# A product-key expert kernel: the first key's one-hots of four tokens from one bf16 comparison and one product

## The chip, the cores and the metric

The kernel runs on one core of a Trainium2 chip. The metric is the device time of one execution in microseconds. Time before: 1866.86 us, the median of 3 runs (1861.45 to 1871.61).

## The reference

One layer of a hybrid encoder over 512 frames of 1024 features (16 learned meta tokens in front, float32 throughout): a mixer (attention with forget gates beside a state space branch), then a channel mixer with 128 x 128 experts, then a norm. The edit lies in the channel mixer, for half of the tokens:

```
s = einsum('bqhjd,hjnd->bqhjn', qry, keys)          # two halves of the key, 128 scores each
v1, i1 = top_k(s[..., 0, :], 16);  v2, i2 = top_k(s[..., 1, :], 16)
best, pos = top_k(v1 + v2 over all 256 pairs, 16)
e1 = i1[pos // 16];  e2 = i2[pos % 16];  gate = softmax(best)
act = gelu(u[e1 * 128 + e2] . x)
out = sum over 8 heads x 16 picks of gate * act * v[e1 * 128 + e2]
```

So each token has 128 picks (8 heads x 16), each with a first key e1, a second key e2 (both 0 to 127) and a gate.

## The kernel before, in words

The kernel is written against the engines directly: five instruction streams (SyncE `sp`, TensorE `pe`, ScalarE `ac`, VectorE `dve`, GpSimd `pool`), each in program order, ordered against each other by semaphores alone. Nothing is scheduled by a planner. The tokens are handled in two halves. The first 256 gather their experts' rows by indirect DMA. The last 256 (HALF) run densely: all 16384 experts are streamed through TensorE in 128 steps, and a table G[first key, second key, token] of gates weighs the activations. `mul(act, act, G[:, n, :])` (the helper at line 1160) does so in step n.

G is built by the loop that the change edits, once both halves' lists are found. Three transposes bring the picks of a token onto the 128 partitions, so that `first_key`, `second_key` and `gate_chosen` hold 256 columns, one a token (ScalarE copies them out of PSUM, `evac`, line 960). For each token TensorE then multiplies two one-hot matrices, 128 picks x 128 keys each: that of the second key, and that of the first key times the gate. The product is the token's 128 x 128 table.

The loop handles four tokens a group, 64 groups, four groups to a turn of the hardware loop `Fori`, so that keys and gates have addresses from the loop's register (`bass.ds(...)`).

- VectorE (lines 1471 to 1482) compares `numbers` (each of 0..127 four times, bf16) with the four tokens' second keys into `marks[b % 2]`, a bf16 tile laid out key by key with the four tokens side by side (128 x 4 = 512 elements), line 1476. Then it waits for `onehot_free` and makes the first key's one-hot times gate into `oh1[:, b]`, float32, one token an instruction, line 1481.
- ScalarE `widen` (line 1105) turns `marks` token by token into float32 `oh2`, reading at a step of four bf16 elements, that is 8 bytes. `read_gates` (line 1109) copies a group's product from PSUM into G.
- TensorE (line 921) waits for room in PSUM (`gmat_free`), for `oh2_ready` and for `oh1_ready`, and multiplies the group's four tokens; a float32 product is two passes, so 8 matmuls a group. Then it raises `onehot_free`.

`onehot_free` starts at 4, `gmat_free` at 4 and `oh2_ready` at 2, so there are four one-hot buffers and four PSUM banks, and two buffers of marks. SyncE waits for `onehot_free` to reach 4 + 64 before the first expert load (lines 469 and 474), since `u_in` and `v_in`, the tiles it loads into, are the same memory as `oh2` and `oh1`.

Of the kernel before, what the change touches and what calls it, by code (L numbers as in the profile page):

```python
# [15 lines left out]
ALU = mybir.AluOpType  # L16
# [3 lines left out]
BF16 = mybir.dt.bfloat16  # L20
# [3 lines left out]
P = 128  # L24
# [20 lines left out]
HALF = SEQ // 2  # L45
# [67 lines left out]
def hybrid_program(nc, x, meta, g_mix, g_ffn, g_ffn_row, g_out, w_u, w_k, w_q, w_v, w_f, w_g, b_f, b_g, w_att, w_val,  # L113
# [12 lines left out]
    for hf in range(2):  # L126
# [18 lines left out]
        a, b = TILES[hf]  # L145
# [9 lines left out]
    for n, (name, where) in enumerate(order):  # L155
        if where == "turn":
            p, turns = turns % 2, turns + 1
        else:
            p = n % 4 if where is None else where
# [3 lines left out]
    with ExitStack() as ctx:  # L163
        sb = lambda name, shape, dt=F32: ctx.enter_context(nc.sbuf_tensor(name, shape, dt))
        sem = lambda name: ctx.enter_context(nc.semaphore(name))
        gate_all = sb("gate_all", [P, G_WORDS])
        chosen = sb("chosen", [P, 3, SEQ])
        cd = sb("cd", [P, 2, NT, 32])
        iota = sb("iota", [P, P])
# [8 lines left out]
        hnT = sb("hnT", [P, DC, L])  # L178
# [12 lines left out]

        act = [hnT[:, b, 0:HALF] for b in range(2)]
        marks = [hnT[:, 4 + b, 0:HALF].bitcast(BF16).rearrange("p (e t) -> p e t", t=4) for b in range(2)]
        numbers = hnT[:, 6, 0:HALF].bitcast(BF16).rearrange("p (e t) -> p e t", t=4)
        gate_sel = hnT[:, 7, 0:HALF]
        idx = chosen[:, 0, 0:HALF].bitcast(U32)
        wsel = chosen[:, 0, HALF:SEQ]
        first_key = chosen[:, 1, 0:HALF]
        second_key = chosen[:, 1, HALF:HALF + HALF // 2].bitcast(BF16)
        gate_chosen = chosen[:, 2, 0:HALF]  # L200
        oh1 = v_in.rearrange("p s (b t e) -> p (s b) t e", b=2, t=4)
# [52 lines left out]
        def lists(base):  # L254
# [64 lines left out]
        gates_raw, gates_exp = sem("gates_raw"), sem("gates_exp")  # L319
        idx_ready, chosen_ready = sem("idx_ready"), sem("chosen_ready")  # L320
        numbers_ready = sem("numbers_ready")
        oh2_marked, oh1_ready, oh2_ready, onehot_free, gmat_free = (
            sem("oh2_marked"), sem("oh1_ready"), sem("oh2_ready"), sem("onehot_free"), sem("gmat_free"))
        sel_gelu, row_done = sem("sel_gelu"), sem("row_done")
        row_landed = [sem(f"row_landed{i}") for i in range(SLOTS)]
        u_landed = [sem(f"u_landed{i}") for i in range(2)]
# [821 lines left out]
        def _(dve):  # L1148
# [79 lines left out]
            for a, (p, q, op) in enumerate((((crb, 0), (cib, 1), ALU.subtract), ((crb, 1), (cib, 0), ALU.add))):  # L1228
# [3 lines left out]
                ins = dve.tensor_tensor(bd[64:P, a, :, GCH:32], bprod[64:P, 0], bprod[64:P, 1], op)  # L1232
# [4 lines left out]
            for g in range(2):  # L1237
                r = slice(64 * g, 64 * g + 64)
                dve.tensor_copy(cd[r, 0, :, GCH * g:GCH * (g + 1)], braw[r, 2])
                ins = dve.tensor_scalar(cd[r, 1, :, GCH * g:GCH * (g + 1)], braw[r, 3], -1.0, None, ALU.mult)  # L1240
# [230 lines left out]
            with dve.Fori(0, HALF // 16) as it:  # L1471
                for b in range(4):
                    g = it * 4 + b
                    dve.wait_ge(oh2_ready, g + 1)
                    key = second_key[:, bass.ds(it * 16 + b * 4, 4)].unsqueeze(1)
                    dve.tensor_tensor(marks[b % 2], numbers, key.to_broadcast([P, P, 4]), ALU.is_equal)\
                       .then_inc(oh2_marked, 1)
                    dve.wait_ge(onehot_free, g + 1)
                    for t in range(4):
                        at = it * 16 + b * 4 + t  # L1480
                        ins = dve.tensor_scalar(oh1[:, b, t], iota[:], first_key[:, bass.ds(at, 1)],  # L1481
                                                gate_chosen[:, bass.ds(at, 1)], ALU.is_equal, ALU.mult)
                    ins.then_inc(oh1_ready, 1)

            def add_residual(g, h, total):
                dve.wait_ge(res_landed[g], 16)
# [77 lines left out]
```

## Time and profile before

| | |
|---|---|
| median of 3 runs | 1866.86 us |
| the profiled execution | 1863.51 us, its span 1861.7 us |
| mean granted TensorE clock | 0.957 of 2.4 GHz |
| TensorE matmuls busy | 1696.2 us (91%) |
| VectorE busy | 1180.9 us (63%) |
| GpSimd busy | 897.8 us (48%) |
| ScalarE busy | 305.0 us (16%) |
| DMA | 489.48 MB, mean 263 GB/s |

The span is the time from the first to the last instruction of the profiled execution; its device time is 1.8 us longer. Busy times are sums over the whole span; the share says nothing about a single stage. In the rows below an instruction stands as: line of the kernel, engine, operation, tile written <- tiles read, shapes, count. PE is TensorE's matmul, PEld its weight load, DVE VectorE, ACT ScalarE, POOL GpSimd, SPq SyncE's queue, DVEq VectorE's sequencer.

### The profile page before, as it was taken

The page shows a single profiled execution, that of the slowest core. Times are in us where ns is not written, and L with a number is a line of the kernel's source. Part 1 is how long each engine was busy: PE and PEld are TensorE (multiplying, and loading weights), DVE is VectorE, ACT ScalarE, POOL GpSimd, SP SyncE. Part 2 cuts the span into 40 slices and gives each one's busy share as a digit, 9 for nine tenths or more (in the row PEclk, how much of TensorE's full clock was granted, in tenths as well). Part 3 has the DMA queues.
Part 4 walks back from the last instruction along what each step waited for, and adds up shares of the span by engine and source line. Part 5 has one row for each costly group of instructions (what it writes and reads, how often), then busy time and mean ns, then how long its engine had stood idle before and what let it go on. Part 6 is the DMA issues. An engine that isn't in the chain of part 4 may idle for free.

```text
span 1861.7 us, 20468 instructions
## 1 busy us (share of the span) xinstructions
PE 1696.2 (91%) x6646; PEld 1165.0 (63%) x6646; DVE 1180.9 (63%) x2636; ACT 305.0 (16%) x718; POOL 897.8 (48%) x1125
## 2 busy tenths in 40 slices
PE   7989999996999968946889999999999999999996
PEld 6456675884556654835766666666666666666664
DVE  4255531696767543799956666666756666666666
ACT  3112231111212311116820000000100000000001
POOL 5954410386666521681034544454545545546442
PEclk9989999997989989987999999999999999999998
DMA  6311145447344493600069999999999999999997
GB/s 228 95 54 57 35 143 174 150 135 292 114 138 134 135 353 133 249 24 0 0 243 409 408 409 409 409 406 409 409 406 409 405 409 397 409 409 404 409 409 296
DMA packets 138092, 489.48 MB, mean 263 GB/s; under 512 B 16384, under 2 KB 16896, under 8 KB 137744
## 3 DMA queue, kind: packets, MB, share of 16 engines
q0 software_dynamic: 73728, 268.47, 37.1%
q1 hardware_dynamic: 64272, 219.85, 31.9%
q8 instruction: 50, 0.82, 0.2%
q14 instruction: 42, 0.34, 0.1%
HBM read 483.53 MB, written 4.72 MB: 262 GB/s over the span
## 4 chain that ended last, share of the span: by engine, by line
DMA 42%; PE 28%; DVE 14%; POOL 9%; issue 4%; ACT 2%; DVEq 0%; SPq 0%; POOLq 0%; ACTq 0%
DMA ring<-in_expert_v,chosen 23%; DMA ring<-in_expert_rows,chosen 17%; PE pair L666 12%; DVE ring L1275 3%; POOL ring L632 3%; DVE ring L1272 2%; PE pair L921 2%; PE pair L699 2%; PE pair L838 1%; PE pair L866 1%; PE pair L722 1%; DMA gate_all<-in_w_val 1%; PE pair L721 1%; DVE temp L1481 1%; PE pair L742 1%
## 5 line engine op out<-in xcount | busy, mean ns | idle before, releaser
L908 PE MATMUL pair<-temp,hnT 128*128 128x512 f32 x1024 | 461.9, 594 | 13.1 <-DVE hnT L1160 12.8
L899 PE MATMUL pair<-hnT,temp 128*128 128x256 f32 x2048 | 465.2, 381 | 3.8 <-DMA temp<-in_expert_u 3.8
L899 PEld LDWEIGHTS pair<-hnT,temp 128*128 128x128 f32 x2048 | 391.2, 191 | 110.8 <-issue 64.1
L632 POOL DMA_INDIRECT ring<-in_expert_rows,chosen x256 | 273.5, 1068 | 384.2 <-DVE ring L1272 346.8
L1275 DVE SCALAR_TENSOR_TENSOR ring<-ring,chosen 128x1024 f32<-128x1024 f32 x256 | 328.9, 1285 | 159.3 <-DMA ring<-in_expert_v,chosen 157.8
L1272 DVE SCALAR_TENSOR_TENSOR ring<-ring 128x1024 f32<-128x1024 f32 x256 | 324.4, 1277 | 144.6 <-DMA ring<-in_expert_rows,chosen 144.0
L632 POOL DMA_INDIRECT ring<-in_expert_v,chosen x256 | 264.4, 1033 | 262.1 <-DVE ring L1275 239.8
L908 PEld LDWEIGHTS pair<-temp,hnT 128*128 128x128 f32 x1024 | 192.9, 190 | 210.1 <-issue 203.1
L1134 ACT ACTIVATE hnT<-pair 128x256 f32<-128x256 f32 x128 | 48.9, 383 | 818.1 <-PE pair L899 818.1
L666 PE MATMUL pair<-hnT,gate_all 128*128 128x256 f32 x576 | 137.8, 396 | 1.4 <-issue 1.4
L666 PE MATMUL pair<-hnT,ring 128*128 128x256 f32 (+1 forms) x512 | 125.6, 406 | 1.5 <-DVE hnT L1160 1.5
L666 PEld LDWEIGHTS pair<-hnT,gate_all 128*128 128x128 f32 x576 | 112.8, 200 | 17.0 <-issue 1.6
L666 PEld LDWEIGHTS pair<-hnT,ring 128*128 128x128 f32 x512 | 102.3, 203 | 18.9 <-issue 2.5
L1334 DVE TENSOR_REDUCE st<-pair 128x1 f32<-128x144 f32 (+3 forms) x32 | 16.2, 507 | 123.7 <-PE pair L723 109.1
L921 PE MATMUL pair<-temp 128*128 128x128 f32 x512 | 73.2, 288 | 13.8 <-DVE temp L1481 13.7
L666 PE MATMUL pair<-hnT,temp 128*128 128x256 f32 x320 | 81.4, 414 | 0.0
L921 PEld LDWEIGHTS pair<-temp 128*128 128x128 f32 x512 | 63.4, 196 | 23.8 <-ACT temp L1105 23.2
L576 POOL TENSOR_TENSOR gate_all<-temp,gate_all 128x256 f32<-128x256 f32 x32 | 23.2, 725 | 111.6 <-DVE temp L1307 111.6
L666 PEld LDWEIGHTS pair<-hnT,temp 128*128 128x128 f32 x320 | 66.0, 210 | 10.2 <-issue 0.2
L1481 DVE TENSOR_SCALAR temp<-iota,chosen 128x128 f32<-128x128 f32 x256 | 70.8, 336 | 0.0
L1160 DVE TENSOR_TENSOR hnT<-hnT,gate_all 128x256 f32<-128x256 f32 x128 | 54.2, 423 | 21.5 <-ACT hnT L1134 19.0
L960 ACT ACTIVATE gate_all<-pair 128x256 f32<-128x256 f32 (+3 forms) x75 | 30.2, 403 | 185.0 <-PE pair L666 152.9
(258 smaller groups left out, 1734.8 us busy)
## 6 DMA issues: line engine op xcount, KB each, us to landing
temp<-in_expert_u SPq DMA_DIRECT2D x128, 512.0 KB, 6.8
temp<-in_expert_v SPq DMA_DIRECT2D x128, 512.0 KB, 6.8
gate_all<-in_w_query SPq DMA_DIRECT2D x24, 512.0 KB, 4.4
ring<-in_w_g SPq DMA_DIRECT2D x16, 512.0 KB, 3.5
ring<-in_w_u SPq DMA_DIRECT2D x8, 512.0 KB, 4.6
ring<-in_w_out SPq DMA_DIRECT2D x8, 512.0 KB, 4.7
temp<-in_w_query SPq DMA_DIRECT2D x8, 512.0 KB, 3.6
ring<-in_expert_rows,chosen POOLq DMA_INDIRECT x256, 10.3
```

Of the source, the lines that this page charges most:

```text
L632: pool.indirect_dma_start(out=gathered[:, g % SLOTS, :], out_offset=None, in_=(expert_rows, expert_v_rows)[part], in_offset=bass.IndirectO ...
L666: mm = pe.matmul(pair(name)[:, 0:width], w[:, c, :], rhs[:, c, lo:lo + width], start=(c == 0), stop=(c == kc - 1))
L699: pe.matmul(pair(name)[:, 0:WIDTH[hf]], bT[q:q + 32, a, i // 4, :], uT[hf][q:q + 32, i // 4, :], start=True, stop=True).then_inc(full_sem( ...
L899: mm = pe.matmul(u_out[n % 2], u_in[:, n % 2, c * P:(c + 1) * P], hnT[:, c, FIRST[1]:L], start=(c == 0), stop=(c == DC - 1))
L908: mm = pe.matmul(pairs[i][:, b * 512:(b + 1) * 512], act[n % 2][:, i * P:(i + 1) * P], v_in[:, n % 2, b * 512:(b + 1) * 512], start=False, ...
L921: mm = pe.matmul(pairs[2 + s // 2][:, (s % 2) * 512 + t * P:(s % 2) * 512 + (t + 1) * P], oh2[s][:, t], oh1[:, s, t], start=True, stop=True)
L960: ac.activation(dst, pair(name)[0:rows, cols[0]:cols[1]], ACT.Copy, scale=scale).then_inc(free_sem(name), 1)
L1134: ac.activation(act[n % 2], u_out[n % 2], ACT.Gelu).then_inc(gelu_done, 1)
L1160: return dve.tensor_tensor(out, a, b, ALU.mult)
L1272: dve.scalar_tensor_tensor(out=slot, in0=slot, scalar=1.0, in1=xrow, op0=ALU.mult, op1=ALU.mult, accum_out=wsel[:, at:at + 1]).then_inc(ro ...
L1275: dve.scalar_tensor_tensor(out=fin, in0=slot, scalar=wsel[:, at:at + 1], in1=fin, op0=ALU.mult, op1=ALU.add).then_inc(row_done, 1)
L1481: ins = dve.tensor_scalar(oh1[:, b, t], iota[:], first_key[:, bass.ds(at, 1)], gate_chosen[:, bass.ds(at, 1)], ALU.is_equal, ALU.mult)
```

## The change

The first key's one-hots are made like the second key's, by a comparison of bf16 tiles into a new pair of buffers, `first_marks`; a second instruction multiplies them by the gates, reading the marks token by token (a step of 8 bytes) and each gate as a value that stands still over 128 keys, and writes the float32 tile of four tokens. Between the two VectorE waits for its own comparison through a new semaphore, `oh1_marked`. `first_key` is held in bf16 (as `second_key` is), in half the room.

```diff
+        first_marks = [hnT[:, 2 + b, 0:HALF].bitcast(BF16).rearrange("p (e t) -> p e t", t=4) for b in range(2)]
...
-        first_key = chosen[:, 1, 0:HALF]
+        first_key = chosen[:, 1, 0:HALF // 2].bitcast(BF16)
...
                     dve.tensor_tensor(marks[b % 2], numbers, key.to_broadcast([P, P, 4]), ALU.is_equal)\
                        .then_inc(oh2_marked, 1)
+                    key = first_key[:, bass.ds(it * 16 + b * 4, 4)].unsqueeze(1)
+                    dve.tensor_tensor(first_marks[b % 2], numbers, key.to_broadcast([P, P, 4]), ALU.is_equal)\
+                       .then_inc(oh1_marked, 1)
+                    dve.wait_ge(oh1_marked, g + 1)
                     dve.wait_ge(onehot_free, g + 1)
-                    for t in range(4):
-                        at = it * 16 + b * 4 + t
-                        ins = dve.tensor_scalar(oh1[:, b, t], iota[:], first_key[:, bass.ds(at, 1)],
-                                                gate_chosen[:, bass.ds(at, 1)], ALU.is_equal, ALU.mult)
-                    ins.then_inc(oh1_ready, 1)
+                    gate = gate_chosen[:, bass.ds(it * 16 + b * 4, 4)].unsqueeze(2).to_broadcast([P, 4, P])
+                    dve.tensor_tensor(oh1[:, b], first_marks[b % 2].rearrange("p e t -> p t e"), gate, ALU.mult)\
+                       .then_inc(oh1_ready, 1)
```

## Rows read from the trace of the kernel before

**Rows 1.** The loop's ends in the timeline, and stretches: us, PE, PEld, DVE, ACT, POOL busy, PEclk.

```profile
851.88 0.43 DVE L1476 TENSOR_TENSOR hnT<-hnT,chosen 128x512 bf16<-128x512 bf16 x1 [2.52 <-ACT chosen L960]
...
939.25 1.13 PE L921 MATMUL pair<-temp 128*128 128x128 f32 x8 [0.23 <-DVE temp L1481]
940.40 0.80 SPq L469 DMA_DIRECT2D temp<-in_expert_u  x2
...
944.17 9.53 PE L899 MATMUL pair<-hnT,temp 128*128 128x256 f32 x32 [3.79 <-DMA temp<-in_expert_u]
...
650.00:660.00 10.00, 5.66 (x26) 4.34 (x24) 4.32 (x9) 2.76 (x8) 2.62 (x2) 0.94 1.05 426
850.00:860.00 10.00, 9.32 (x61) 8.40 (x59) 8.12 (x30) 6.94 (x13) 0.00 (x0) 0.66 0.00 1
860.00:900.00 40.00, 33.05 (x235) 28.36 (x235) 40.00 (x148) 34.03 (x60) 0.00 (x0) 1.00 0.00 0
```

**Rows 2.** Timeline of one group in the loop: start us, us, instruction, idle before.

```profile
861.42 0.41 DVE L1476 TENSOR_TENSOR hnT<-hnT,chosen 128x512 bf16<-128x512 bf16 x1
861.61 0.97 PEld L921 LDWEIGHTS pair<-temp 128*128 128x128 f32 x8 [0.40 <-ACT temp L1105]
861.64 1.13 PE L921 MATMUL pair<-temp 128*128 128x128 f32 x8 [0.24 <-DVE temp L1481]
861.76 1.10 DVE L1481 TENSOR_SCALAR temp<-iota,chosen 128x128 f32<-128x128 f32 x4
861.86 0.69 ACT L1105 ACTIVATE temp<-hnT 128x512 f32<-128x512 bf16 x1 [0.20 <-DVE hnT L1476]
862.45 0.58 ACT L1109 ACTIVATE gate_all<-pair 128x512 f32 x1
862.78 0.41 DVE L1476 TENSOR_TENSOR hnT<-hnT,chosen 128x512 bf16<-128x512 bf16 x1
```

**Rows 3.** Waits from 855 to 940 us: us in total, times, longest.

```profile
PE pair L921 <- DVE temp L1481: 13.7, 59, 0.2
ACT temp L1105 <- DVE hnT L1476: 12.5, 61, 0.7
```

**Rows 4.** VectorE's instructions by line and shape, whole span: busy us, mean ns.

```profile
L1481 DVE TENSOR_SCALAR temp<-iota,chosen 128x128 f32<-128x128 f32 x256 | 70.8, 336 | 0.0
L1160 DVE TENSOR_TENSOR hnT<-hnT,gate_all 128x256 f32<-128x256 f32 x128 | 54.2, 423 | 21.5 <-ACT hnT L1134 19.0
L1476 DVE TENSOR_TENSOR hnT<-hnT,chosen 128x512 bf16<-128x512 bf16 x64 | 26.4, 413 | 2.5 <-ACT chosen L960 2.5
...
L1160 DVE TENSOR_TENSOR hnT<-pair,gmix 128x1024 f32<-128x1024 f32 x4 | 4.8, 1221 | 3.8 <-PE pair L657 3.8
...
L1169 DVE TENSOR_SCALAR temp<-temp,st 128x1024 f32<-128x1024 f32 x4 | 3.0, 754 | 0.1
...
L1412 DVE TENSOR_REDUCE gate_all<-gate_all 128x32 f32<-128x512 bf16 x2 | 2.0, 1006 | 0.1
```

**Rows 5.** Register instructions of lines 1476 and 1481: ns min/median/max, first and last start.

```profile
L1476 DVEq FUSED_REGOPS  x64: 65/65/76, 851.8 to 936.1; - x64
...
L1481 DVEq FUSED_REGOPS  x256: 93/93/104, 851.9 to 936.8; - x128
```

**Rows 6.** Timeline ahead of the loop, VectorE's own chain.

```profile
841.58 0.73 DVE L1160 TENSOR_TENSOR gate_all<-gate_all 128x512 bf16<-128x512 bf16 x1
...
847.87 0.42 DVE L1446 TENSOR_REDUCE gate_all<-gate_all 128x16 f32<-128x256 f32 x1
...
848.32 0.25 DVE L1447 RECIPROCAL gate_all<-gate_all 128x16 f32<-128x16 f32 x1
```

**Rows 7.** ScalarE's instructions by line and shape, whole span: busy us, mean ns.

```profile
L1134 ACT ACTIVATE hnT<-pair 128x256 f32<-128x256 f32 x128 | 48.9, 383 | 818.1 <-PE pair L899 818.1
L1105 ACT ACTIVATE temp<-hnT 128x512 f32<-128x512 bf16 x64 | 43.5, 680 | 14.2 <-DVE hnT L1476 14.2
...
L949 ACT ACTIVATE temp<-temp 128x1024 f32<-128x1024 f32 x4 | 4.2, 1057 | 61.2 <-DVE temp L1368 61.2
```

More of the change, by code:

```diff
@@ L321, in hybrid_program @@
         numbers_ready = sem("numbers_ready")
-        oh2_marked, oh1_ready, oh2_ready, onehot_free, gmat_free = (
-            sem("oh2_marked"), sem("oh1_ready"), sem("oh2_ready"), sem("onehot_free"), sem("gmat_free"))
+        oh1_marked, oh2_marked, oh1_ready, oh2_ready, onehot_free, gmat_free = (
+            sem("oh1_marked"), sem("oh2_marked"), sem("oh1_ready"), sem("oh2_ready"), sem("onehot_free"), sem("gmat_free"))
         sel_gelu, row_done = sem("sel_gelu"), sem("row_done")
```

## The prediction

> **What bounds the kernel now.** I read the page's engine shares first, then the groups of instructions, and then the loop of the edit in order of time. Over the whole span TensorE is busiest, but the edit touches one loop alone, so its limit is read from that stretch. The loop runs from the first comparison at 851.88 us to the last matmuls at 939.25 + 1.13 = 940.38 us; at 940.40 SyncE issues the first expert load, and TensorE waits for it until 944.17 [rows 1]. SyncE is held by `onehot_free` until the last matmul group is done, because the loads land on the tiles that hold the one-hots. So each microsecond that the loop gains or loses moves everything behind it.
>
> The loop handles 64 groups of four tokens. One group in order of time [rows 2]: VectorE compares for the second key (0.41 us), then makes four small one-hots for the first key (1.10 us together); ScalarE widens (0.69) and reads the product (0.58); TensorE multiplies (1.13 from first to last). The next comparison begins 862.78 - 861.42 = 1.36 us later. VectorE never pauses: its four small instructions begin at 861.76, 0.34 us after the comparison, though that lasts 0.41, so neighbours overlap by 0.07 us; four at 255 ns from start to start (1.10 = 3 x 0.255 + 0.336) make 1.02, and 0.34 + 1.02 = 1.36. The waits say the same: TensorE waits on the four instructions 0.23 us a group, ScalarE on the comparison 0.20 us a group [rows 3]. ScalarE could do a group in 1.36 - 0.20 = 1.16 us and TensorE in 1.36 - 0.23 = 1.13. VectorE sets the pace, with 0.2 us of air under it. Check: 64 x 1.36 = 87.0 us against 88.5 from first comparison to last matmul.
>
> **The change part by part, per group.**
>
> *Removed:* four TENSOR_SCALAR of 128x128, 336 ns each by the row [rows 4], 1.02 us of VectorE's pace.
>
> *Added, the first comparison of the first key:* the same form as the existing one (bf16 tiles of 512, 413 ns by the row [rows 4]). The existing comparison in front of it now costs 0.34 to the start of its follower. The new one is followed by a wait for its own result, so it costs its full 0.41.
>
> *Added, the wait.* The product can't start until the new comparison has signalled. Behind it on VectorE stand the product and then everything of the next group; behind them TensorE, which needs the product, and ScalarE, which needs the next comparison. Where the trace has an instruction that waits for its predecessor on VectorE, the gap is 0.03 us (a reduction ends at 847.87 + 0.42 = 848.29, its reader starts at 848.32 [rows 6]). That is the lower bound, 0.035. But here the product's gate operand has an address from the loop counter, and the trace shows a register instruction in front of each such instruction: 65 ns in front of the comparison, 93 ns in front of a small one with two such operands [rows 5]. Today they run ahead while VectorE is busy and cost nothing. Behind a wait one of them is exposed: the wait stands in front of it, in program order. The first one starts at 851.8 and lasts 76 ns, and its comparison starts at 851.88; I estimate 0.115 us from its start to the start of the instruction, and 0.035 + 0.115 = 0.15 us of gap. There are two waits in front of the product; if both cost in turn it is some 0.25 us (my upper bound: 0.15 plus another 0.1). I take 0.15. Its cover is gone by construction: nothing is queued between the comparison and its reader.
>
> *Added, the product.* 512 elements, one bf16 operand read at a step of 8 bytes, one float32 operand that stands still over 128 elements, float32 out. The trace doesn't show this operation. Float32 TENSOR_TENSORs take 423 ns for 256 elements and 1221 ns for 1024 [rows 4], so 1.04 ns an element and 157 ns fixed; the 1024 one has just such an operand that stands still over a run, and pays nothing for it. For 512 this gives 0.69. The nearest row in types, a bf16 tile of 512 times a float32 operand, took 0.73 [rows 6]. Lower bounds: 0.50 if it ran at the rate of the float32 TENSOR_SCALAR (754 ns for 1024, [rows 4], against 336 for 128, 0.47 ns an element), 0.41 if at that of the all-bf16 comparison. Upper bound: 1.01 from the reduction that reads 512 bf16 elements 64 bytes apart [rows 4]; a reduction of 256 contiguous ones takes 0.42 [rows 6], so with the same 157 ns fixed the far step makes 1.66 ns an element against 1.03. The step here is 8 bytes, not 64. The row with exactly this pattern is ScalarE's widening: 680 ns for 512, where its 256 takes 383 and its 1024 takes 1057 [rows 7]; by these 0.88 ns an element and 158 fixed, so the strided read runs at (680 - 158) / 512 = 1.02 ns an element. That is just VectorE's own pace, so I expect no surcharge there, and take the 0.73 of the nearest row. The overlap with its follower, 0.07 to 0.08, leaves 0.65.
>
> The Trainium skill has two pages on that step, and they disagree. "Vector Engine (DVE) Microarchitecture Reference", section 5.2, says a port keeps its full rate only while it reads runs of two adjacent 4-byte words, and lists 1.73 ns a column for one source that hops every element: 512 of them and the fixed part of the rows would make the product 1.04 us. "SBUF — State Buffer", section Specifications, has lines of 16 bytes and asks for two hits in each for full rate, which a step of 8 bytes gives: 0.69. ScalarE's row speaks for the second, the reduction's row allows the first.
>
> *Moved or nothing:* the register instructions of the three that remain are fewer than the five before; after the product they have its 0.65 us to run ahead. ScalarE writes the first key in bf16 once, no more elements than before. The comparison's tiles are double and VectorE is in order, so no wait for a free buffer is added. The loads, the gathers (POOL idle in this stretch) and the whole last stage are as before, only later.
>
> **The sum.** Group: 0.336 + 0.413 + 0.15 + 0.65 = 1.549 us against 1.362, so +0.187. The two comparisons and the product alone, 1.40, already equal what they replace; the exposed wait makes the loss. 64 groups: +12.0 us. The profiled execution took 1863.5 us (span 1861.7 and 1.8 around it); it becomes 1875.5. The median of the runs shown is 3.3 us above it, so 1866.9 + 12.0 = 1878.9.
>
> **Rivals.**
> - *A, the product runs at a faster mode (not slower than before).* Place: the product. If it costs 0.41 (0.34 to its follower), the group is 0.336 + 0.413 + 0.15 + 0.34 = 1.24, -0.12 us, -8 us: 1859. With the 0.50 of the other bound the group is 1.33 and the kernel at 1865. It decides from a product under 0.53 us on. For it: single-source float32 instructions do run twice as fast [rows 4]. Against: every TENSOR_TENSOR with a float32 operand in the trace runs at 1.04 ns an element. Floor in any case: ScalarE's 1.16, -13 us. Chance 0.08.
> - *B, the wait costs almost nothing.* The gap is the 0.035 of a plain chained instruction, since the register instruction runs ahead of the wait: group 1.43, or 1.39 with the product at 0.69; +2 to +5 us, 1869 to 1871. For it: chained gaps on the page are that short. Against: in program order the wait comes first, and a sequencer that holds there can't have run what is behind. Chance 0.17.
> - *C, the strided read is slow.* Product 1.01 us, 0.93 to its follower: group 0.336 + 0.413 + 0.15 + 0.93 = 1.83, +30 us: 1897. For it the reduction, against it ScalarE on this very pattern. The microarchitecture page named above would make it 1.86 and 1899. Chance 0.20.
> - *D, TensorE's clock.* TensorE is busy 33.05 of 40 us in the loop now, at full clock (2.4 GHz); with a group of 1.55 it would be 73% busy. In the stretch 650 to 660, busy 5.66 of 10 us, the clock had begun to fall, to a mean of 0.94 [rows 1]. At 1.2 GHz a group's eight passes, now (1.13 - 0.28) / 7 = 0.12 us apart, would take up to 8 x 0.24 = 1.94 us, and TensorE would set the pace: +37 us at most if it stayed there, 1904. But at that rate it has no pause left, and in the loop's first 10 us the clock rose from such a start (mean 0.66) to 1.00 [rows 1]. Chance 0.05, and then mostly a few us on top.
>
> The forecast itself has 0.50.
>
> **How the numbers follow.** About 0.5% (9.3 us) is what a measurement of this kernel can tell from no change. The forecast's own range, product 0.69 to 0.75 us and gap 0.15 to 0.25, is a group of 1.51 to 1.67, +9.7 to +20 us: 1877 to 1887. Its low end lies on that line, so of its 0.50 I count 0.42 as slower and 0.08 as within. Slower: 0.42 + C 0.20 + 0.03 of D = 0.65. Within: 0.08 + B 0.17 + half of A 0.04 + 0.02 of D = 0.31. Faster: 0.04, the other half of A. The range, 1867 to 1898, leaves out A, the lowest of B, the highest of C and the worst of D.
>
> **What would show it.** In the changed profile: (1) two comparisons a group of 0.41 us, the second starting 0.34 after the first; (2) a pause of VectorE in front of the product of about 0.15 us, whose releaser is VectorE itself; (3) the product near 0.73 us; (4) a group of 1.55 us, TensorE and ScalarE waiting about 0.4 us each a group; (5) the stages in front of 851 and behind the loop unchanged in length. The prediction is wrong if the group stays at 1.36 to 1.43 (B), falls under it (A), or the product takes over 0.9 us (C); and it is wrong in its frame if the loop's change isn't handed on to the end one for one.

## The result and the profile after

The changed kernel takes 1877.09 us (median of 12 runs, 1873.39 to 1882.9) against 1865.68 us for the kernel before (12 runs, 1859.44 to 1871.91). The ratio is 1.0055, 95% interval 1.0042 to 1.0069: slower by 10.3 us, between 7.8 and 12.9 (the two medians are 11.4 us apart). One run in the experiments, of 2979.1 us at a mean granted clock of 0.551 where all others have 0.951 to 0.958, is a slow one: it enters no ratio, though the median of 1862.04 us of the swapped kernel counts it. The profiled execution of the changed kernel took 1877.84 us. Its span, the engines' busy time and the granted clock in 40 slices, from the page of the changed kernel:

```profile
span 1876.0 us, 20276 instructions
...
PE 1701.7 (91%) x6646; PEld 1165.5 (62%) x6646; DVE 1183.1 (63%) x2508; ACT 305.2 (16%) x718; POOL 897.6 (48%) x1125
...
PEclk9989899998988989978999999999999999999998
```

VectorE has 128 instructions fewer (2508 against 2636) and 2 us more busy time over the whole span; in the loop itself the three rows below sum to 97.8 us against 97.2 [rows 4], so the loss isn't in its busy time. The loop in order of time, the first group's three VectorE instructions and then one whole group (the changed kernel's lines: 1477 is the second key's comparison, 1480 the first key's, 1485 the product, 1106 ScalarE's widening, 1110 its reading of the product, 922 TensorE):

```profile
857.69 0.42 DVE L1477 TENSOR_TENSOR hnT<-hnT,chosen 128x512 bf16<-128x512 bf16 x1 [2.51 <-ACT chosen L961]
...
858.03 0.42 DVE L1480 TENSOR_TENSOR hnT<-hnT,chosen 128x512 bf16<-128x512 bf16 x1
...
858.59 0.69 DVE L1485 TENSOR_TENSOR temp<-hnT,chosen 128x512 f32<-128x512 bf16 x1
...
862.20 0.42 DVE L1477 TENSOR_TENSOR hnT<-hnT,chosen 128x512 bf16<-128x512 bf16 x1
862.39 0.97 PEld L922 LDWEIGHTS pair<-temp 128*128 128x128 f32 x8 [0.53 <-ACT temp L1106]
862.43 1.13 PE L922 MATMUL pair<-temp 128*128 128x128 f32 x8 [0.37 <-DVE temp L1485]
862.53 0.42 DVE L1480 TENSOR_TENSOR hnT<-hnT,chosen 128x512 bf16<-128x512 bf16 x1
862.65 0.68 ACT L1106 ACTIVATE temp<-hnT 128x512 f32<-128x512 bf16 x1 [0.34 <-DVE hnT L1477]
863.09 0.69 DVE L1485 TENSOR_TENSOR temp<-hnT,chosen 128x512 f32<-128x512 bf16 x1
863.24 0.57 ACT L1110 ACTIVATE gate_all<-pair 128x512 f32 x1
863.70 0.42 DVE L1477 TENSOR_TENSOR hnT<-hnT,chosen 128x512 bf16<-128x512 bf16 x1
```

A group is now 863.70 - 862.20 = 1.50 us, against 1.36 in [rows 2]. The second comparison starts 0.33 us after the first, and ends at 862.53 + 0.42 = 862.95. Nothing runs on VectorE until 863.09: that is the pause, 0.14 us. The product lasts 0.69, and the next comparison starts 0.61 after it began. 0.33 + 0.42 + 0.14 + 0.61 = 1.50.

The end of the loop, and VectorE's groups of instructions there (idle time of the engine before them behind the second bar):

```profile
953.96 1.13 PE L922 MATMUL pair<-temp 128*128 128x128 f32 x8 [0.37 <-DVE temp L1485]
955.12 0.80 SPq L470 DMA_DIRECT2D temp<-in_expert_u  x2
...
958.79 6.50 PE L900 MATMUL pair<-hnT,temp 128*128 128x256 f32 x16 [3.71 <-DMA temp<-in_expert_u]
```

```profile
L1485 DVE TENSOR_TENSOR temp<-hnT,chosen 128x512 f32<-128x512 bf16 x64 | 44.3, 692 | 8.9
L1477 DVE TENSOR_TENSOR hnT<-hnT,chosen 128x512 bf16<-128x512 bf16 x64 | 26.8, 418 | 2.5 <-ACT chosen L961 2.5
L1480 DVE TENSOR_TENSOR hnT<-hnT,chosen 128x512 bf16<-128x512 bf16 x64 | 26.7, 418 | 0.0
```

The loop runs from 857.69 to 953.96 + 1.13 = 955.09 us: 97.4 us against 88.5 in [rows 1]. The product's row has 8.9 us of idle time in front of it, 0.14 a group, where the row of the four small instructions had 0.0 [rows 4]; the page names no releaser for it. Two waits stand in front of the product, for `oh1_marked` (VectorE's own comparison) and for `onehot_free`; which of them it is, the experiments tell. TensorE's and ScalarE's waits from 855 to 950 us, answering to [rows 3], and the loop's two stretches, answering to [rows 1]:

```profile
PE pair L922 <- DVE temp L1485: 22.7, 61, 0.4
ACT temp L1106 <- DVE hnT L1477: 22.7, 62, 1.0
```

```profile
860.00:900.00 40.00, 29.96 (x214) 25.61 (x213) 36.31 (x80) 30.47 (x53) 0.00 (x0) 1.00 0.00 0
900.00:950.00 50.00, 37.75 (x269) 32.44 (x270) 45.42 (x101) 38.65 (x67) 0.00 (x0) 1.00 0.00 0
```

TensorE waits 22.7 us for the product, 0.37 a group, ScalarE for the comparison as much, and TensorE is busy 29.96 of 40 us, 75%. The granted clock is 1.00 in both stretches, the level of 2.4 GHz.

The profiled span is 14.3 us longer, more than the medians say. Of that 5.8 us lie in front of the loop (it starts at 857.69 instead of 851.88), where no instruction was changed; 8.9 us in the loop; -0.4 us behind it (1876.0 - 955.1 = 920.9 against 1861.7 - 940.4 = 921.3). Over the nine kernels profiled here the loop starts anywhere from 851.9 to 861.5 us, so what lies in front is the spread between executions.

### The profile page after: what moved, and what is told of

The parts are those of the page before. It is cut to its first block, busy times and chain, and to the rows that moved or that the text cites. A ratio compares the mean times of both kernels' runs of the same rounds, so it can differ in the third digit from the quotient of the medians.

```text
span 1876.0 us, 20276 instructions
## 1 busy us (share of the span) xinstructions
PE 1701.7 (91%) x6646; PEld 1165.5 (62%) x6646; DVE 1183.1 (63%) x2508; ACT 305.2 (16%) x718; POOL 897.6 (48%) x1125
## 4 chain that ended last, share of the span: by engine, by line
DMA 41%; PE 30%; DVE 15%; issue 5%; POOL 5%; ACT 2%; DVEq 1%; SPq 0%; POOLq 0%; ACTq 0%
DMA ring<-in_expert_v,chosen 23%; DMA ring<-in_expert_rows,chosen 16%; PE pair L667 14%; DVE ring L1276 3%; POOL ring L633 3%; DVE ring L1273 2%; PE pair L700 2%; PE pair L723 1%; PE pair L839 1%; PE pair L867 1%; PE pair L722 1%; DVE hnT L1480 1%; PE pair L743 1%; PE pair L687 1%; DVE hnT L1477 1%
## 5 line engine op out<-in xcount | busy, mean ns | idle before, releaser
L909 PE MATMUL pair<-temp,hnT 128*128 128x512 f32 x1024 | 462.2, 594 | 11.4 <-DVE hnT L1161 10.9
L633 POOL DMA_INDIRECT ring<-in_expert_v,chosen x256 | 260.2, 1017 | 265.5 <-DVE ring L1276 241.3
L667 PE MATMUL pair<-hnT,ring 128*128 128x256 f32 (+1 forms) x512 | 131.0, 418 | 1.5 <-DVE hnT L1161 1.5
L667 PEld LDWEIGHTS pair<-hnT,ring 128*128 128x128 f32 x512 | 106.1, 211 | 20.5 <-issue 2.5
L1161 DVE TENSOR_TENSOR gate_all<-pair,gate_all 128x256 f32<-128x256 f32 x32 | 13.6, 424 | 64.9 <-PE pair L667 56.8
## 6 DMA issues: line engine op xcount, KB each, us to landing
ring<-in_expert_rows,chosen POOLq DMA_INDIRECT x256, 10.3
```

What stands on the lines that cost most here:

```text
L633: pool.indirect_dma_start(out=gathered[:, g % SLOTS, :], out_offset=None, in_=(expert_rows, expert_v_rows)[part], in_offset=bass.IndirectO ...
L667: mm = pe.matmul(pair(name)[:, 0:width], w[:, c, :], rhs[:, c, lo:lo + width], start=(c == 0), stop=(c == kc - 1))
L909: mm = pe.matmul(pairs[i][:, b * 512:(b + 1) * 512], act[n % 2][:, i * P:(i + 1) * P], v_in[:, n % 2, b * 512:(b + 1) * 512], start=False, ...
L1161: return dve.tensor_tensor(out, a, b, ALU.mult)
```

## The experiments

Theory W: the new instructions by themselves are no dearer than those they replace, and the loss is VectorE's wait for its own comparison: a pause of 0.14 us a group, most of it a register instruction that the wait exposes, and the 0.08 us by which the comparison no longer overlaps its follower. The rivals, one letter each, are named in each expectation.

**The first key's comparison in front.** The two comparisons of a group are swapped, nothing else:

```diff
+                    key = first_key[...]
+                    dve.tensor_tensor(first_marks[b % 2], numbers, ...).then_inc(oh1_marked, 1)
                     key = second_key[...]
                     dve.tensor_tensor(marks[b % 2], numbers, ...).then_inc(oh2_marked, 1)
-                    key = first_key[...]
-                    dve.tensor_tensor(first_marks[b % 2], numbers, ...).then_inc(oh1_marked, 1)
                     dve.wait_ge(oh1_marked, g + 1)
```

> The changed kernel with the two comparisons of a group swapped: the first key's stands first, so the second key's runs between it and the wait in front of the product. Nothing is added or removed. Theory W (the loss is the exposed wait): the product's register instruction and semaphore pass under the second key's comparison; a group is 0.334 + 0.334 + 0.610 = 1.28 us against 1.50 in the changed kernel and 1.362 before, the loop 64 x 1.28 = 82 us, the kernel 64 x 0.084 = 5.4 us under the kernel before (about 1860, ratio 0.997), and 14 us under the changed one. Rival P (the loss is in the new instructions themselves, the comparison and the product are dearer in sum than the four small ones): the order doesn't matter, group 1.50, ratio 1.0055. Rival L (VectorE's gain is not handed on because ScalarE or TensorE then sets the pace): group between 1.28 and 1.36 with a pause of VectorE, ratio 0.998 to 1.000.

Measured: ratio to the kernel before 0.9972, interval 0.9958 to 0.9986; 1862.04 us against 1868.24. One group in order of time (1477 is here the first key's comparison, 1480 the second's):

```profile
864.96 0.42 DVE L1477 TENSOR_TENSOR hnT<-hnT,chosen 128x512 bf16<-128x512 bf16 x1
...
865.20 0.97 PEld L922 LDWEIGHTS pair<-temp 128*128 128x128 f32 x8 [0.30 <-ACT temp L1106]
865.29 0.42 DVE L1480 TENSOR_TENSOR hnT<-hnT,chosen 128x512 bf16<-128x512 bf16 x1
865.63 0.68 DVE L1485 TENSOR_TENSOR temp<-hnT,chosen 128x512 f32<-128x512 bf16 x1
865.74 0.68 ACT L1106 ACTIVATE temp<-hnT 128x512 f32<-128x512 bf16 x1
866.23 0.42 DVE L1477 TENSOR_TENSOR hnT<-hnT,chosen 128x512 bf16<-128x512 bf16 x1
```

A group is 866.23 - 864.96 = 1.27 us. 865.29 + 0.42 = 865.71 lies behind 865.63, the product's start: the pause is gone, and the product comes 0.34 us after the comparison in front of it, as any neighbour does. Theory W held, P fell: the same instructions in another order are 15 us apart by the ratios (1.0055 - 0.9972 = 0.0083 of 1868). L fell too: nothing stops VectorE. The wait for `onehot_free` stands in this kernel as before and costs nothing, so the pause was the wait for `oh1_marked`.

**Both comparisons in one instruction, a group ahead.**

```diff
...
+            both_keys = chosen[:, 1, :].bitcast(BF16).rearrange("p (k n) -> p k n", k=2)
+            both_numbers = numbers.unsqueeze(2).to_broadcast([P, P, 2, 4])
+
+            def compare(g, at, b):
+                dve.wait_ge(oh2_ready, g + 1)
+                key = both_keys[:, :, at].unsqueeze(1)
+                dve.tensor_tensor(both_marks[b], both_numbers, key.to_broadcast([P, P, 2, 4]), ALU.is_equal)\
+                   .then_inc(oh2_marked, 1)
+
+            def weigh(g, at, b):
+                dve.wait_ge(oh2_marked, g + 1)
...
+            compare(0, slice(0, 4), 0)
...
+                    compare(it * 4 + b + 1, bass.ds(it * 16 + b * 4 + 4, 4), (b + 1) % 4)
+                    weigh(it * 4 + b, bass.ds(it * 16 + b * 4, 4), b)
```

> Both keys' comparisons of a group in one instruction of 1024 bf16 elements (two keys' rows by a step of the key operand and of the marks tile), issued one group ahead of the product that reads it; four buffers for the first key's marks. Theory W and the rows' rates: comparison 0.157 + 1024 x 0.5 = 0.68 us, 0.61 to its follower, product 0.61 to its follower, group 1.22 us, 64 x -0.147 = -9.4 us against before: about 1856, ratio 0.995; ScalarE, which can do a group in 1.16, then pauses 0.05. Rival R (the joined operand with one more dimension falls out of the fast bf16 rate): comparison 0.157 + 1024 x 1.04 = 1.22 us, group 1.76, ratio 1.014. Rival L (ScalarE's wait for the comparison plus its two instructions turn it into the pace-setter): group about 1.3.

Measured: ratio 0.9937, interval 0.9919 to 0.9955; 1855.16 us, the fastest kernel of the study, 0.63% under the kernel before. In order of time (1480 the joined comparison, 1487 the product), and the loop's stretch as in [rows 1]:

```profile
862.75 0.68 DVE L1487 TENSOR_TENSOR temp<-hnT,chosen 128x512 f32<-128x512 bf16 x1
862.92 0.68 ACT L1106 ACTIVATE temp<-hnT 128x512 f32<-128x512 bf16 x1
863.35 0.69 DVE L1480 TENSOR_TENSOR hnT<-hnT,chosen 128x1024 bf16<-128x1024 bf16 x1
...
863.63 0.60 ACT L1110 ACTIVATE gate_all<-pair 128x512 f32 x1
863.95 0.68 DVE L1487 TENSOR_TENSOR temp<-hnT,chosen 128x512 f32<-128x512 bf16 x1
```

```profile
860.00:900.00 40.00, 37.53 (x267) 32.21 (x267) 40.00 (x67) 38.88 (x68) 0.00 (x0) 1.00 0.00 0
```

A group is 863.95 - 862.75 = 1.20 us (1.22 expected). The joined comparison lasts 0.69, so (0.69 - 0.16) / 1024 = 0.52 ns an element: it kept the fast rate, and R fell; so did L, since the group isn't 1.3 and VectorE has no pause. The joining and the issue a group ahead were not tried apart; by the rows the joining saves 0.07 us (0.60 from start to start against two of 0.33), and the swap alone had already hidden the wait. The other two engines are now near their limits as well: in 40 us ScalarE is busy 38.88, TensorE 37.53, VectorE all of it. So this is about the end of what VectorE's side can give.

**The wait alone.** The kernel before and one line more:

```diff
                        .then_inc(oh2_marked, 1)
+                    dve.wait_ge(oh2_marked, g + 1)
                     dve.wait_ge(onehot_free, g + 1)
```

> The kernel before, its four small instructions a group kept, with nothing added but VectorE's wait for its own comparison of the second key in front of them (a wait that the data doesn't need). Theory W: the comparison costs its full 0.413 in place of 0.336, and the first small instruction's register instruction (93 ns, in place of the product's 53) is exposed, a gap of 0.17 us: group 1.362 + 0.077 + 0.17 = 1.61 us, +16 us, ratio 1.0085. Rival G (the gap is that of a plain chained instruction, 0.035): group 1.47, +7 us, ratio 1.004. Rival P (waits on its own engine cost nothing): ratio 1.000.

Measured: ratio 1.0101, interval 1.0077 to 1.0125, that is +18.9 us (14 to 23); expected were +16. In order of time:

```profile
862.25 0.42 DVE L1476 TENSOR_TENSOR hnT<-hnT,chosen 128x512 bf16<-128x512 bf16 x1
...
862.85 1.12 DVE L1482 TENSOR_SCALAR temp<-iota,chosen 128x128 f32<-128x128 f32 x4 [0.18 <-DVE hnT L1476]
...
863.88 0.42 DVE L1476 TENSOR_TENSOR hnT<-hnT,chosen 128x512 bf16<-128x512 bf16 x1
```

862.25 + 0.42 = 862.67, and the first small instruction starts at 862.85: a pause of 0.18 us (0.17 expected), and a group of 1.63 us against 1.36, 64 x 0.27 = 17 us. A wait that the data doesn't need, put in front of instructions that were running without a pause, costs more than the whole change did. G and P fell. Here the view names the releaser of the pause, VectorE's own comparison in line 1476, and nothing but the wait for it was added.

**A gate at a fixed address.** The product's gate operand is `gate_chosen[:, b * 4:b * 4 + 4]` instead of an address from the loop's register; the gates used are wrong ones.

> The changed kernel with the product's gate operand at a fixed address (the first 16 tokens' gates for all; the values are wrong, the shapes are the same), so that no register instruction stands between the wait and the product. Theory W with the register instruction as most of the gap: gap 0.035 to 0.05 us in place of 0.138, group 1.40 to 1.41, 6 us under the changed kernel, +2.5 us against before, ratio 1.0015. Rival S (the gap is the semaphore, not the register instruction): group stays at 1.50, ratio 1.0055.

Measured: ratio 1.0011, interval 0.9997 to 1.0025. In order of time:

```profile
862.52 0.42 DVE L1477 TENSOR_TENSOR hnT<-hnT,chosen 128x512 bf16<-128x512 bf16 x1
...
862.86 0.42 DVE L1480 TENSOR_TENSOR hnT<-hnT,chosen 128x512 bf16<-128x512 bf16 x1
...
863.31 0.69 DVE L1485 TENSOR_TENSOR temp<-hnT,chosen 128x512 f32<-128x512 bf16 x1
...
863.92 0.42 DVE L1477 TENSOR_TENSOR hnT<-hnT,chosen 128x512 bf16<-128x512 bf16 x1
```

862.86 + 0.42 = 863.28, and the product starts at 863.31: the pause is 0.03 us, the plain chained gap of [rows 6]. The group is 1.40. So of the 0.14 us some 0.10 are the register instruction behind the wait and its way to the engine, and S fell. The changed kernel's trace shows it in place: in the first group the comparison ends at 858.03 + 0.42 = 858.45, the product's register instruction starts at 858.5 (its row is under the next heading) and the product at 858.59. In the swapped kernel the first of these register instructions starts at 859.0 as well, when the first key's comparison ends (858.58 + 0.43 = 859.01), but the second key's runs from 858.92 to 859.34 and covers it. What is left against before, 1.40 - 1.36 = 0.04 us a group, is that 0.03, the 0.08 of overlap that the wait costs and 0.01 by which the product lasts longer behind a pause (0.691 against 0.683 in the swapped kernel), less the 0.09 (1.36 - 1.27) by which the new instructions are cheaper when nothing is exposed, as the swapped kernel showed.

**The step of the product's read.** Three kernels differ from the changed one in how the product walks over its 512 marks; the one-hots that come out are wrong ones in all three. Contiguous, and nothing else changed:

```diff
-                    dve.tensor_tensor(oh1[:, b], first_marks[b % 2].rearrange("p e t -> p t e"), gate, ALU.mult)\
+                    dve.tensor_tensor(oh1[:, b], first_marks[b % 2].rearrange("p (t e) u -> p t (e u)", t=4), gate, ALU.mult)\
```

> The changed kernel with the product reading the marks in the order in which they lie (consecutive bf16 elements) instead of at a step of 8 bytes; the one-hots come out in the wrong order, all shapes stay. Theory N (the 8-byte step costs nothing on VectorE, the product is a plain 1.04 ns an element): product 691 ns as in the changed kernel, group 1.50 us. Rival H (part of the 691 ns is the step): product shorter, down to 0.41 us if the read alone set the rate.

At 16 bytes, by `rearrange("p (w k) -> p k w", w=64)` over the same 512 elements, read as 8 rows of 64, with one gate that stands still over all 512:

> The changed kernel with the product reading the marks at a step of 16 bytes (64 elements, then the next of 8 such rows) and one gate for the whole group; values wrong, the count of elements the same. Theory N with a line of 16 bytes: every element is on a line of its own, so the surcharge begins here: product 0.157 + 512 x 1.66 = 1.01 us (the rate of the reduction in the rows of before), group 1.83. Rival F (it begins only at a farther step): product 691 ns, group 1.50.

At 64 bytes, the same with `w=16`, that is 32 rows of 16:

> As the run at 16 bytes, at a step of 64 bytes (16 elements, then the next of 32 such rows), which is the reduction's step in the kernel before. Theory N: product 1.01 us, group 1.83 us, about +21 us on the changed kernel, which is what the rival C of the prediction would have cost. Rival T (the reduction was slow because it is a reduction, not by its step): product 691 ns, group 1.50.

The product's row of the changed kernel with its register instruction (ns min/median/max, first and last start), and then the product's row of the contiguous kernel, of the one at 16 bytes and of the one at 64 bytes:

```profile
L1485 DVEq FUSED_REGOPS  x64: 53/53/53, 858.5 to 953.0; - x64
L1485 DVE TENSOR_TENSOR temp<-hnT,chosen x64: 691/691/694, 858.6 to 953.1; 128x512 f32<-128x512 bf16 x64
```

```profile
L1485 DVE TENSOR_TENSOR temp<-hnT,chosen x64: 691/691/694, 854.6 to 949.1; 128x512 f32<-128x512 bf16 x64
```

```profile
L1486 DVE TENSOR_TENSOR temp<-hnT,chosen x64: 1054/1072/1081, 862.4 to 980.6; 128x512 f32<-128x512 bf16 x64
```

```profile
L1486 DVE TENSOR_TENSOR temp<-hnT,chosen x64: 1009/1019/1026, 857.1 to 972.0; 128x512 f32<-128x512 bf16 x64
```

691 ns contiguous and 691 ns at 8 bytes: the step of the change is free (theory N; H fell). At 16 bytes 1072 ns (1.01 us expected), at 64 bytes 1019: with the 157 ns fixed, 1.79 and 1.68 ns an element (F and T fell). At 64 bytes the rate is that of the reduction of [rows 4] at the same step, 1.66. Each of the three ran once: 1874.08, 1904.28 and 1896.11 us beside 1870.16 for the kernel before; their loops are 97.4, 121.5 and 118.1 us long. The farther step of the two is the cheaper one, and no run tells why: the rows are of 64 elements in one and of 16 in the other, so step and row length changed together. That the one gate costs nothing is assumed, since it was not varied alone.

## Why the prediction was right

It forecast 1878.9 us and +12.0; measured were 1877.1 and +10.3 (7.8 to 12.9). The mechanism came out as told, the wait and its register instruction; the closeness of the time is in part luck, since the loop, where the forecast put all of its +12.0, grew by 8.9. Point by point:

- *VectorE sets the loop's pace, and the loop's change is handed on one for one.* Shown. From the first expert load's issue to the end of the span it is 921.3 us before, 920.9 after, 920.2 in the swapped kernel (941.49 to 1861.7), 919.4 in the joined one (931.86 to 1851.3), while their loops are 88.5, 97.4, 82.9 and 78.7 us long.
- *Two comparisons of 0.41, the first overlapped by 0.07.* Right: 0.417 and 0.335 to the follower.
- *A pause of 0.15, from 0.035 of semaphore and 0.115 for the register instruction.* Measured 0.138. The split was right as well: without the register instruction the pause is 0.034. Of the two waits in front of the product the one for `onehot_free` was free, as the swapped kernel shows.
- *The product at 0.73.* The mis-sized term: 0.691. The fit through the float32 rows (157 + 512 x 1.04) had said 0.69, and I took the nearest row by types instead, 0.73 [rows 6]. That was no clean price: GpSimd was at work beside it, and the same form took 1.47 us at 845.32 us, beside a GpSimd instruction of 1.21; whether GpSimd made it longer no run tells. This is 0.04 of the 0.05 us a group by which the forecast was too long: 1.549 against 1.500.
- *Nothing for the 8-byte step.* Shown by the contiguous kernel. Beforehand it was an inference from another engine: 1.02 ns an element for ScalarE on the same pattern against VectorE's 1.04, though ScalarE's rate by its other rows was 0.88. Rival C's product would have come true at a step of 16 bytes. The Trainium skill's "SBUF — State Buffer", section Specifications, says that a line of 16 bytes wants two hits for full rate; the trace agrees with it, 691 ns at 8 bytes and 1072 at 16, steps between them not tried. The Trainium skill's "Vector Engine (DVE) Microarchitecture Reference", section 5.2, gives 1.73 ns for one source that hops at every element, there with 4-byte words, which is near the 1.79 and 1.68 at 16 and 64 bytes. Its rule of two adjacent 4-byte words would have charged the 8-byte step too, and for the bf16 read here the measurement decides against that.
- *Rival A* needed a product under 0.53 us: no sign of it. (Its bound of 0.50 should have been 336 + 384 x 0.47 = 516 ns, which changes nothing.) *Rival B* is what the fixed-address kernel did, a pause of 0.03. *Rival D*: TensorE busy 75% of the time from 860 to 950 us, and the granted clock at 1.00 in that stretch.

The sum said that the two comparisons and the product, 1.40, already equal what they replace, 1.36. That holds only with the wait's lost overlap counted to them. By themselves, as the swapped kernel runs them, a group is (938.8 - 858.6) / 63 = 1.273 us (first and last start of its line 1477), 0.09 cheaper than the 1.362 before; the wait adds 0.23 to reach 1.501: 0.083 of overlap, 0.138 of pause and 0.008 of the longer product.

By sizes: the group's 1.501 - 1.362 = 0.139 us x 64 = +8.9 us, as the loop's +8.9. The ratio's +10.3 holds that in its interval.

What I missed is that the loss could be had back for nothing. The prediction called the wait's cover "gone by construction", since nothing is queued between the comparison and its reader; but the other comparison stood right there to be queued. Swapped, the change is a gain of 5.2 us (2.6 to 7.8).

## What to carry to other kernels

Fewer, larger instructions are worth the difference of their start-to-start times (here 5.6 us of the loop), and one wait of an engine for its own last result can cost more than that (here 14.5 us, 97.4 against 82.9). Put an independent instruction between the two. The wait cost more where the instruction behind it has an address from a register (a pause of 0.138 us against 0.034), because the sequencer's work for it then lay bare too. And before pricing a strided read, look for a row of any engine that already reads in that pattern.

## What the runs showed of the hardware that was not expected

- VectorE neighbours without a wait between them overlap by 0.08 us here. With a wait for the first one's result there is a pause of 0.034 us with fixed addresses, 0.138 with one register address (53 ns of register instruction) and 0.18 with two (93 ns).
- The same product lasts 683 ns where it overlaps the instruction in front of it and 691 behind a pause.
- An all-bf16 TENSOR_TENSOR of 1024 elements in runs of four, with one operand standing still over two rows and the output in two places, keeps 0.52 ns an element.
- A product of a bf16 tile with a float32 operand costs VectorE 1.04 ns an element where the bf16 read is contiguous or at a step of 8 bytes, 1.79 at 16 bytes and 1.68 at 64 (the last two in one run each, with shorter rows).
